# Hybrid encoder layer with expert-choice FFN: stationary blocks of 96 instead of 128 columns in the expert stage

## The reference

```
h = rms_norm(x);  p = h @ w_in                       # 1024 -> 3104 columns
x = x + concat(gated_linear_attention(p), diff_attention(p)) @ w_out
h = rms_norm(x)
aff = softmax(h @ w_router)                          # 16 experts
gates, idx = top_k(aff.T, cap)                       # cap = 32 (prompt), 64 (sample)
xe = h[idx]                                          # the rows that an expert picked
ye = (silu(xe @ w_gate) * (xe @ w_up)) @ w_down      # 1024 -> 2048 -> 1024
x = x + scatter_add(ye * gates)
```

## Time and profile before

| | us |
|---|---|
| median of 3 runs | 1552.11 (1551.42 to 1552.47) |
| the profiled execution's own time | 1552.91 |
| its span, first to last instruction | 1551.1 |
| TensorE matmul busy | 1492.5 (96%), 7228 matmuls |
| TensorE weight load busy | 1221.5 (79%) |
| VectorE busy | 1252.7 (81%) |
| ScalarE busy | 1065.4 (69%) |
| GpSimd busy | 127.7 (8%) |
| mean granted TensorE clock | 0.985 |

### The profile page before, as it was taken

One profiled execution on the slowest core, in us unless ns is written; L12 is line 12 of the kernel. 1 busy time (PEld: TensorE's weight loads), 2 busy tenths in 40 slices (PEclk: granted clock), 3 DMA queues, 4 the chain that ended last, 5 costly groups with the idle time before them and its releaser, 6 DMA issues.

```text
span 1551.1 us, 18383 instructions
## 1 busy us (share of the span) xinstructions
PE 1492.5 (96%) x7228; PEld 1221.5 (79%) x7228; DVE 1252.7 (81%) x1144; ACT 1065.4 (69%) x1133; POOL 127.7 (8%) x103
## 2 busy tenths in 40 slices
PE   6998998999949999999999999999999999999997
PEld 5786777667838888888888888888888888888885
DVE  5359588786478898988889898888989888898985
ACT  7434335676347778787877877787787877778784
POOL 1023122000000001000000000000000101000000
PEclk9999999999969999999999999999999999999999
DMA  7111011401749999999999999999999999999992
GB/s 244 55 55 55 1 55 55 151 28 55 258 138 373 390 356 387 386 378 395 378 394 378 384 386 376 395 375 394 380 384 388 375 394 379 391 383 381 393 375 65
DMA packets 192069, 448.49 MB, mean 289 GB/s; under 512 B 12976, under 2 KB 13296, under 8 KB 191984
## 3 DMA queue, kind: packets, MB, share of 16 engines
q1 hardware_dynamic: 187440, 433.03, 74.9%
q0 software_dynamic: 3968, 12.65, 3.6%
q10 hardware_dynamic: 576, 1.64, 0.3%
HBM read 434.71 MB, written 12.58 MB: 288 GB/s over the span
## 4 chain that ended last, share of the span: by engine, by line
PE 90%; DVE 5%; issue 2%; ACT 1%; DMA 1%; POOL 0%; POOLq 0%; DVEq 0%; ACTq 0%
PE ps L910 23%; PE ps L912 23%; PE ps L911 23%; PE ps L591 5%; PE ps L593 5%; PE ps L592 5%; PE ps L945 1%; PE ps L806 1%; PE ps L840 1%; DVE t L1445 1%; DVE states L1430 1%; PE ps L903 1%; PE ps L826 1%; PE ps L862 1%; DMA ident<-in_ident 0%
## 5 line engine op out<-in xcount | busy, mean ns | idle before, releaser
L1752 DVE TENSOR_TENSOR wl<-raw,wh 128x2048 fp32r<-128x2048 f32 x384 | 873.5, 2290 | 127.6 <-ACT wh L1279 126.2
L1279 ACT CAST wh<-raw 128x2048 fp32r<-128x2048 f32 x384 | 731.2, 1913 | 127.6 <-PE ps L912 125.4
L910 PE MATMUL ps<-wh,XTh 128*128 128x512 f32 x1024 | 405.9, 396 | 0.6 <-issue 0.6
L912 PE MATMUL ps<-wl,XTh 128*128 128x512 f32 x1024 | 400.3, 391 | 0.0
L911 PE MATMUL ps<-wh,XTl 128*128 128x512 f32 x1024 | 399.5, 390 | 0.0
L912 PEld LDWEIGHTS ps<-wl,XTh 128*128 128x128 f32 x1024 | 192.8, 188 | 41.3
L910 PEld LDWEIGHTS ps<-wh,XTh 128*128 128x128 f32 x1024 | 192.9, 188 | 38.9 <-issue 0.9
L911 PEld LDWEIGHTS ps<-wh,XTl 128*128 128x128 f32 x1024 | 193.1, 189 | 38.3
L910 PE MATMUL ps<-wh,gTh 128*128 128x512 f32 x512 | 200.9, 392 | 1.2 <-DVE gTl L1763 1.2
L912 PE MATMUL ps<-wl,gTh 128*128 128x512 f32 x512 | 199.4, 390 | 0.0
L911 PE MATMUL ps<-wh,gTl 128*128 128x512 f32 x512 | 199.2, 389 | 0.0
(11 more groups left out here) (238 smaller groups left out, 1519.3 us busy)
## 6 DMA issues: line engine op xcount, KB each, us to landing
raw<-in_w_gate SPq DMA_DIRECT2D x128, 1024.0 KB, 11.0
raw<-in_w_up SPq DMA_DIRECT2D x128, 1024.0 KB, 11.5
raw<-in_w_down SPq DMA_DIRECT2D x128, 1024.0 KB, 11.4
slice_raw<-in_w_in SPq DMA_DIRECT2D x6, 2048.0 KB, 8.0
X<-in_x_sample SPq DMA_DIRECT2D x8, 512.0 KB, 12.6
slice_raw<-in_w_out SPq DMA_DIRECT2D x2, 2048.0 KB, 9.2
X<-in_x_prompt SPq DMA_DIRECT2D x4, 512.0 KB, 5.0
h_rows<-hn SPq DMA_DIRECT2D x4, 512.0 KB, 3.3
```

The lines of the kernel that those rows point to most:

```text
L910: pe.matmul(out, hi, rhs_h, start=first, stop=False)
L912: return pe.matmul(out, hi, rhs_l, start=False, stop=last)
L1279: act.copy(wh[:, n % CONV, :], raw[:, n % RAW, :]).then_inc(s_wh, 1)
L1752: dve.tensor_tensor(wl[:, n % CONV, :], raw[:, n % RAW, :], wh[:, n % CONV, :].bitcast(F32), ALU.subtract).then_inc(s_wl, 1)
```

## The change

The helper's stationary operands and outputs are cut to the 96 columns (CAP) that hold data. The tiles keep their shape, so that blocks still begin 512 bytes apart. The clears, their semaphore and TensorE's wait go.

```diff
-        s_pad = sem("spare_columns_cleared")
...
-            pool.wait_ge(s_lg, NT)
-            pool.memset(XTh[0][:, :, CAP:P].bitcast(F32), 0.0)
-            pool.memset(XTl[0][:, :, CAP:P].bitcast(F32), 0.0)
-            pool.memset(gTh[:, :, CAP:P].bitcast(F32), 0.0)
-            pool.memset(gTl[:, :, CAP:P].bitcast(F32), 0.0).then_inc(s_pad, 1)
             for b in range(2):
                 pool.wait_ge(s_h2w[b], 16 * (NT // 2))
-            pool.memset(XTh[1][:, :, CAP:P].bitcast(F32), 0.0)
-            pool.memset(XTl[1][:, :, CAP:P].bitcast(F32), 0.0).then_inc(s_pad, 1)
             pool.wait_ge(s_route, 1)
...
-                        mm = products(ps[:, b, :], (XTh[j][:, kk, :], XTl[j][:, kk, :]),
+                        mm = products(ps[0:CAP, b, :], (XTh[j][:, kk, 0:CAP], XTl[j][:, kk, 0:CAP]),
                                       h_[:, k, :], l_[:, k, :], kk == 0, kk == KD - 1)
...
-                        mm = products(ps[:, 4 + half, :], (gTh[:, ff, :], gTl[:, ff, :]),
+                        mm = products(ps[0:CAP, 4 + half, :], (gTh[:, ff, 0:CAP], gTl[:, ff, 0:CAP]),
                                       h_[:, f, d], l_[:, f, d], s == 0 and ff == 0,
                                       s == NS - 1 and ff == FC - 1)
...
-            pe.wait_ge(s_pad, 2)
```

## The result

The changed kernel takes 1561.84 us (median of 4 runs, 1561.23 to 1563.81) against 1552.29 us of the kernel before (4 runs): ratio 1.0066, 95% interval 1.0054 to 1.0077. It is slower by 9.6 us; the forecast was 1550.0 and its range ended at 1553.5. The profiled execution took 1561.86 us, 8.95 us more than before's, with a span of 1560.0.

What follows compares the result with a forecast made beforehand. TensorE was taken as the bound, at 0.2267 us a matmul step in the expert stage. Only the exposed loads counted, -2.1 us from the median of 1552.11, giving 1550.0 us; range 1546.5 to 1553.5.

Steps and rivals of the forecast that it cites:

- (a): Loading a stationary block in the expert stage: 96 columns take an estimated 161 ns, 27 ns less than 128.
- (b): The 4,608 expert-stage loads hidden behind 512-column matmuls: shortening them changes 0; ends -14.3 and +18.4 us.
- (c): Loads exposed behind groups of transposes: 80 of them, 26.5 ns less each, 2.1 us saved; bounds 0 and 4.2 us.
- nothing: Rival, 13%: the 0.11 us behind transposes is no load time or returns as a wait; median stays 1552.1 us.
- (d): Removing six GpSimd clears, semaphore and wait: value 0, covered by GpSimd's wait for the routing table before the first gather.
- (e): What a faster TensorE meets: ScalarE, VectorE and DMA keep up in the expert stage, so nothing is late next.
- the step grows: Rival, 6%: every expert-stage step stays in the 0.231 us state, 18.4 us less 2.1, giving 1568.4 us.
- the slow steps go too: Rival, 16%: the seven longer steps behind each group of transposes vanish, 2.1 us more saved, 1547.9 us.
- The two rules: Faster 128-column load lost at 96 (1556.3 us, 1%); array emptied when widths alternate between transposes and products (1578 us, 1%).

Runs made afterwards that it cites:

- widths run: Kernel before with another stationary width for each expert, 128 down to 32 columns: mean step 227.2 ns at 128, 227.3 at 113, up to 236.1 at 117.
- place runs: Kernel before with stationary blocks starting at another column of their 128-column place per expert: steps of 229.6, 233.3 and 230.4 ns at 112 columns, 227.2 at 128.
- quiet run: Experts at 96, 128, 120 or 113 columns, with weight conversions, weight loads or both cut short: step 230.0 ns all four times at 96, 233.3 at 120.
- narrow-block run: Kernel before with transposes moved one split product later and only the block exposed behind them cut to 96 columns: 1548.55 us, ratio 0.9978 to its control without the cut.

## Why the prediction was wrong, point by point

- **(a) the load of 96 columns**: right. 161 was said, 162 ns measured.
- **(b) the hidden loads: the step that failed.** It took 0 for the 4,608 hidden loads, with +4.0 ns as the upper end; the step grew by 3.3 ns (0.2267 to 0.2300), 2.7 ns on average over the stage, which is +12.1 us. The argument was that a load that ends before the next matmul can't set the step. The widths and the place runs show that width and address of a block matter while its load is hidden; the quiet run shows that conversions and loads from HBM have no part in it. What failed in the reading: the gate projection's mean of 0.2307 was the row of the same moving width, and it was set aside because steps of that length also occur at 128 columns. They occur there in the first ten steps behind transposes and then stop (226.7 from the eleventh on); in the gate projection steps of 224 to 238 ns follow each other to the end of the stretch. The mean was the measurement, and the widths run agrees with it: 231.6 at 32 columns and 230.1 at 64.
- **(c) the exposed load**: right in mechanism and size (80 x 28 ns = 2.2 us against 2.1), seen after the change and, by itself, in the narrow-block run. The rival "nothing" took the whole 0.11 us for a fixed delay, and that is excluded; that some 82 ns of it don't shrink further was seen only in the widths run, and 96 columns just reach that floor.
- **(d) the clears**: right, 0, by the run that kept them.
- **(e) nothing is late next**: right; ScalarE's conversions still wait for TensorE alone.
- **The rivals.** What happened is "the step grows", which had 6%; its price was 18.4 us less 2.1, 1568.4. It came out at 1561.84 because the growth was 3.3 ns and not 4.0 (3 us), because it swallows the slow spells (before had 0.6 ns of them in its average step, after has none: 3 us), and in the profiled pair because the stage began 1.0 us to the good. The rival "the slow steps go too" was thus right as an effect and wrong in its sign: they went as all steps became long. In the narrow-block run a part of them did go with a gain.
- **The two rules**: no sign of a faster load lost (162 ns lies on the line of the earlier trace rows) or of an emptied array (a transpose starts 0.23 us behind the last product, as before).

What stays open is why load and stream fall into a step of 226.7 ns at 128 and 113 columns and, on average, of 227.8 to 236.1 elsewhere. A phase between load and stream fits the saw-tooth, the two states at 127 and at 88 columns, the part of the address and the spells behind transposes; this is argued, and no run looked at it directly.

## What to carry to other kernels

A hidden load is not free of effect: where TensorE is the bound, measure the start-to-start step of the very pair of stationary and moving widths, at its own addresses and behind its own transposes, over some tens of matmuls, and count its mean, not its quick ones. Taking columns off a stationary block pays where its load is exposed, behind short matmuls such as transposes, and here only down to 96 columns; do it there alone, and keep the stream's blocks at a width whose step has been measured.

## What the runs showed of the hardware that was not expected

- At full clock the step over 512 moving columns is 226.7 to 236.1 ns by the stationary width, so 13.3 to 22.7 ns above 213.3 (512 columns at 2.4 GHz). At the lower clock level it is 0.42 to 0.43 us at 96 columns (four steps from 456.25 to 457.95 us) as at 128, no more than 512 columns at 1.2 GHz. The Trainium skill gives the columns over 2.4 GHz plus about 2.5 ns as the gap of a single matmul, 216 ns here, and about 131 ns for a sustained stream of loads and matmuls (TensorE: Matmul & The Clock Gate, Back-to-back issue gap). The measurement decides: with a new block for each matmul no width of these runs came near either.
- From 128 down to 96 columns an exposed load costs 0.8 to 0.9 ns a column, and below 96 nothing more is gained (109, 83 and 82 ns from load to load at 128, 96 and 64 columns). The Trainium skill puts a load at 1/1.2 ns a column (TensorE: Matmul & The Clock Gate, LDWEIGHTS (loading the stationary operand)). The trace agrees from 128 to 96 columns; for what follows below, no run shows the cause.
- Blocks 384 bytes apart in SBUF in place of 512 cost 1.4 ns a step at 96 columns, 6 us in this kernel.
- The step is a state that a stream of matmuls keeps: 127 columns ran at 226.7 ns behind 128 columns and at 233.3 behind transposes, 88 columns at 233.3 behind 96 and later at 226.7.
